# x's first four tiles updated ahead of the last output half's copy, and the norm sums ahead of the spectrum products

## What is computed

```python
for l in range(DEPTH):                                   # DEPTH = 2
    h = rms_norm(x, norm1) * (1 + sc1) + sh1
    ... = split(h @ w_in)                                # attention, Hyena and retention branches
    # Hyena: long convolution with a filter that depends on weights alone
    filt = hyena_filter(...); y = irfft(rfft(u) * rfft(filt))
    x = x + g1 * (merged @ w_out)
    h2 = rms_norm(x, norm2) * (1 + sc2) + sh2
    x = x + g2 * moe(h2, ...)                            # top-1 group, top-2 of its 4 experts
y = rms_norm(x, final_g)
```

## Time and profile before

| | us |
|---|---|
| median of 3 runs | 1156.74 (1155.05 to 1159.61) |
| profiled execution, first to last instruction (span) | 1155.5 |
| TensorE busy in it | 1100.4 (95%) |
| VectorE busy | 542.0 (47%) |
| ScalarE busy | 209.8 (18%) |

### The profile page before, as it was taken

One profiled execution on the slowest core, in us unless ns is written; L12 is line 12 of the kernel. 1 busy time (PEld: TensorE's weight loads), 2 busy tenths in 40 slices (PEclk: granted clock), 3 DMA queues, 4 the chain that ended last, 5 costly groups with the idle time before them and its releaser, 6 DMA issues.

```text
span 1155.5 us, 15668 instructions
## 1 busy us (share of the span) xinstructions
PE 1100.4 (95%) x6026; PEld 783.7 (68%) x6026; DVE 542.0 (47%) x1202; ACT 209.8 (18%) x440; POOL 41.0 (4%) x83
## 2 busy tenths in 40 slices
PE   6999999999999999999889999999999999999965
PEld 4688888878887445454358888888888844545422
DVE  2469887677846311121244886646543551111003
ACT  3251022232021101111025111323201210000001
POOL 1001110000000000000000111000000000000000
PEclk9999999999998999999999999999999899999999
DMA  9657865467587999999955677437347979999993
GB/s 382 284 204 279 326 221 227 168 270 272 219 350 318 419 420 422 420 421 421 421 219 201 215 276 285 174 133 283 139 145 306 375 305 421 421 420 421 421 420 121
DMA packets 56943, 351.38 MB, mean 304 GB/s; under 512 B 7088, under 2 KB 7264, under 8 KB 20512
## 3 DMA queue, kind: packets, MB, share of 16 engines
q1 hardware_dynamic: 52704, 337.75, 73.5%
q0 software_dynamic: 4160, 12.58, 3.0%
HBM read 346.08 MB, written 2.65 MB: 302 GB/s over the span
## 4 chain that ended last, share of the span: by engine, by line
PE 84%; DMA 8%; DVE 3%; SPq 3%; ACT 1%; issue 1%; DVEq 0%; ACTq 0%
PE bank L836 26%; PE bank L1127 15%; PE bank L1016 7%; PE bank L1148 6%; DMA ring<-in_experts 5%; PE bank L1037 5%; PE bank L831 5%; PE bank L1112 5%; PE bank L1169 3%; PE bank L847 3%; DMA ring<-in_weights 3%; SPq L615 2%; PE bank L760 1%; PE bank L820 1%; PE bank L961 1%
## 5 line engine op out<-in xcount | busy, mean ns | idle before, releaser
L836 PE MATMUL bank<-h,ring 128*128 128x256 f32 x1472 | 324.8, 380 | 0.0
L836 PEld LDWEIGHTS bank<-h,ring 128*128 128x128 f32 x1472 | 277.4, 190 | 40.1 <-issue 3.2
L1750 DVE SCALAR_TENSOR_TENSOR ring<-ring 128x1024 f32<-128x1024 f32 x160 | 189.5, 1222 | 18.7 <-DMA ring<-in_mod_weights 9.1
L1127 PE MATMUL bank<-ring,gates 128*32 128x512 f32 (+2 forms) x616 | 137.7, 614 | 8.8 <-DMA h<-in_experts 5.0
L1127 PEld LDWEIGHTS bank<-ring,gates 128*32 128x32 f32 (+2 forms) x616 | 41.2, 126 | 69.5 <-issue 69.1
L1127 PE MATMUL bank<-lent,gates 128*32 128x512 f32 (+2 forms) x408 | 81.4, 593 | 2.0 <-ACTq L1618 2.0
L2238 DVE COPY uc_zt_dsum<-bank 128x512 f32<-128x512 f32 x14 | 9.7, 692 | 122.8 <-PE bank L1148 122.8
L1148 PE MATMUL bank<-ring,gates 128*32 128x512 f32 (+1 forms) x240 | 64.4, 595 | 2.0 <-issue 1.2
L1148 PE MATMUL bank<-lent,gates 128*32 128x512 f32 (+2 forms) x304 | 60.5, 594 | 1.3 <-DMA ring<-in_experts 1.0
L1112 PE MATMUL bank<-uc_zt_dsum,gates 128*128 128x128 f32 x448 | 55.5, 285 | 1.0 <-DVEq L2246 1.0
L1127 PEld LDWEIGHTS bank<-lent,gates 128*32 128x32 f32 (+2 forms) x408 | 25.2, 123 | 46.2 <-issue 43.7
(11 more groups left out here) (271 smaller groups left out, 1203.7 us busy)
## 6 DMA issues: line engine op xcount, KB each, us to landing
ring<-in_experts SPq DMA_DIRECT2D x93, 1024.0 KB, 19.8
ring<-in_weights SPq DMA_DIRECT2D x85, 1024.0 KB, 7.7
lent<-in_experts SPq DMA_DIRECT2D x72, 1024.0 KB, 17.8
ring<-in_mod_weights SPq DMA_DIRECT2D x80, 512.0 KB, 5.1
h<-in_experts SPq DMA_DIRECT2D x10, 1024.0 KB, 19.4
uc_zt_dsum<-in_experts SPq DMA_DIRECT2D x10, 1024.0 KB, 19.5
va_vr<-in_experts SPq DMA_DIRECT2D x7, 1024.0 KB, 12.2
lent<-in_weights SPq DMA_DIRECT2D x3, 1024.0 KB, 23.5
```

What stands on the lines that cost most here:

```text
L836: last = pe.matmul(bank[b][:, c * TOK:(c + 1) * TOK], w[:, k, c * P:(c + 1) * P], h[:, k, :], start=(k == 0), stop=(k == KT - 1))
L1127: last = pe.matmul(bank[b][rows, :], hgat[:, 4 * half + f, rows], w[j][:, f, :], start=(half == 1 and f == 0), stop=(half == 0 and f == 3) ...
L1750: last = dve.scalar_tensor_tensor(out, w, 0.5, cond_wide[:, c, :], ALU.mult, ALU.mult, accum_out=mod_all[:, of, row, c:c + 1])
```

## The change

There are three edits. On TensorE, `norm_sum(1)` directly follows the last combine of layer 0; the first two pairs of spectrum products stand behind it, and the third behind `first_units`. On VectorE, x's updates move ahead of the jump, and those of banks 0 and 1 ahead of the copy of the last output half. For this the blocks of further experts, which add to banks 0 to 3 later, start their sums afresh (`True` in place of `False`) and update x once more each; their semaphore counts six events in place of five. The counts of `s_bank_free` for banks 0 to 3 now come ahead of the jump, too.

```diff
+            def spectrum_sum(layer, b, taps_cos, taps_back):
+
+                pe.wait_ge(s_taps, 2 * layer + 2)
+                take(b)
+                pe.matmul(bank[b][:, :], C(taps_cos), hs[:, 0, :], start=True, stop=False)
+                pe.matmul(bank[b][:, :], C(taps_back), hs[:, 1, :], start=False,
+                          stop=True).then_inc(s_spectrum_sum, 1)
...
                 else:
+                    spectrum_sum(layer, 5, "cf", "cf1")
+                    spectrum_sum(layer, 6, "s0", "s1")
                     first_units(layer)
+                    spectrum_sum(layer, 7, "nq", "nq1")
...
                 on = nc.switch_bb(f"pe_on{layer}")
-                if layer + 1 < DEPTH:
-                    filter_step(layer + 1, 4)
             norm_sum(DEPTH)
...
-                        for b in range(4, 8):
+                        for b in range(8):
                             pe.wait_ge(s_bank_free[b], taken[b])
...
-                out_high(PAIRS)
+
+                def moved(b):
+
+                    src = tiles(b)
+                    for c in range(2):
+                        t = 2 * b + c
+                        for g in range(GROUPS):
+                            last = stt(x[:, t, g_cols(g)], src[:, c, g_cols(g)],
+                                       mod_all[:, layer, 40 + t, g:g + 1], x[:, t, g_cols(g)], ALU.mult,
+                                       ALU.add)
+                    return last
+
+                for b in range(4):
+                    if b == 2:
+                        out_high(PAIRS)
+                    dve.wait_ge(s_combined, combined(layer, PAIRS + b + 1))
+                    moved(b).then_inc(s_x_moe, 1)
+                for b in range(4):
+                    dve.wait_ge(s_x_moe, 4 * layer + b + 1)
+                    dve.sem_inc(s_bank_free[b], 1)
...
                     dve.wait_ge(s_more_combined[layer], n + 1)
+                    for b in range(4):
+                        link(moved(b))
+                    dve.sem_inc(s_more_by_vector[layer], 1)
...
                 on = nc.switch_bb(f"dve_on{layer}")
-                for b in range(4):
-                    dve.wait_ge(s_combined, combined(layer, PAIRS + b + 1))
-                    src = tiles(b)
-                    for c in range(2):
-                        t = 2 * b + c
-                        for g in range(GROUPS):
-                            last = stt(x[:, t, g_cols(g)], src[:, c, g_cols(g)],
-                                       modT[:, 40 + t, g:g + 1], x[:, t, g_cols(g)], ALU.mult,
-                                       ALU.add)
-                    last.then_inc(s_x_moe, 1)
-                for b in range(4):
-                    dve.wait_ge(s_x_moe, 4 * layer + b + 1)
-                    dve.sem_inc(s_bank_free[b], 1)
```

More of the change, by code:

```diff
@@ L333, in trunk_program @@
         s_more_known = sem("more_known")
-        s_more_by_vector = [sem(f"more_picked_hgat_act_actT_y{n}") for n in range(DEPTH)]
+        s_more_by_vector = [sem(f"more_picked_hgat_act_actT_y_moved{n}") for n in range(DEPTH)]
         s_more_used = [sem(f"more_used{n}") for n in range(DEPTH)]
@@ L1183, in loaded @@
                     return more[part % 2]
-                pe.wait_ge(s_more_by_vector[layer], 5 * n + 1)
+                pe.wait_ge(s_more_by_vector[layer], 6 * n + 1)
                 for g in range(GROUPS):
@@ L1193, in more_block @@
                 last.then_inc(s_more_gathered[layer], 1)
-                pe.wait_ge(s_more_by_vector[layer], 5 * n + 2)
+                pe.wait_ge(s_more_by_vector[layer], 6 * n + 2)
                 for part in range(4):
@@ L1200, in more_block @@
                     last.then_inc(s_more_used[layer], 1)
-                pe.wait_ge(s_more_by_vector[layer], 5 * n + 3)
+                pe.wait_ge(s_more_by_vector[layer], 6 * n + 3)
                 for f in range(4):
@@ L1204, in more_block @@
                 last.then_inc(s_more_turned[layer], 1)
-                pe.wait_ge(s_more_by_vector[layer], 5 * n + 4)
+                pe.wait_ge(s_more_by_vector[layer], 6 * n + 4)
                 for part in range(4, 6):
@@ L1211, in more_block @@
                     last.then_inc(s_more_used[layer], 1)
-                last = combine(s_more_by_vector[layer], 5 * n + 5, s_more_by_vector[layer],
-                               5 * n + 5, s_more_by_vector[layer], scat[0], False)
+                last = combine(s_more_by_vector[layer], 6 * n + 5, s_more_by_vector[layer],
+                               6 * n + 5, s_more_by_vector[layer], scat[0], True)
                 last.then_inc(s_more_combined[layer], 1)
+                pe.wait_ge(s_more_by_vector[layer], 6 * n + 6)
             pe.wait_ge(s_ones_set, 2)
@@ L1368, in more_block @@
             def more_block(layer, i):
-                sc_e.wait_ge(s_more_by_vector[layer], 5 * i + 1)
+                sc_e.wait_ge(s_more_by_vector[layer], 6 * i + 1)
                 e = sc_e.value_load(ints[0:1, 1:2], min_val=0, max_val=N_EXPERTS - 1)
@@ L1382, in more_block @@
                     s_more_tanh[layer], 1)
+                sc_e.wait_ge(s_more_by_vector[layer], 6 * i + 6)
             sc_e.wait_ge(s_shared_in, 16)
```

## The result

| | before | changed |
|---|---|---|
| median of 6 runs, us | 1155.19 (1154.36 to 1159.61) | 1149.45 (1148.37 to 1152.93) |
| ratio, 95% interval | | 0.9944, 0.9927 to 0.9961 |
| profiled execution, span | 1155.5 | 1148.3 |

The medians differ by 5.7 us; the forecast was 5.9. The time forecast was 1150.9 us and 1149.45 was measured: the gain fits, and the 1.45 us between the two come from the starting point, since the median before is 1.55 us lower over these six runs (1155.19) than over the three that the forecast started from (1156.74). The ratio stands for 6.5 us with an interval of 4.5 to 8.4, and two later groups of runs of the same kernel gave 0.9938 (0.9922 to 0.9953) and 0.9942 (0.9930 to 0.9954). The two profiled executions differ by 7.2 us, which is more than the sum, so the profile has to say where.

What follows compares the result with a forecast made beforehand. Bound: the chain through the seam between layers, where TensorE idles 4.05 us and its clock then falls. 3.43 + 1.69 + 0.74 = 5.86 us off the 1155.5 span, plus 1.2 around it: 1150.9 us, range 1147.9 to 1154.2.

Steps and rivals of the forecast that it cites:

- the sum: Whole kernel: the gains of order, clock and early updates together, 5.86 us.
- The seam: Between the layers, last combine of layer 0 to layer 1's third unit: 25.0 us instead of 30.1.
- C: Rival at the seam: the idle stretch costs more than in this profile, so more is gained; 1149.6 us, chance 0.12.
- B: Rival at the seam: the clock falls anyway; gain 4.2 us, time 1152.6, chance 0.13.
- the clock: Layer 1's first projections: full clock, because TensorE idles about 0.8 us instead of 4.05; gain 1.69 us.
- the order: Seam: norm sums follow the combine, two product pairs fill the norm's stretch, the third costs 1.72; gain 3.43 us.
- The early updates: End of layer 1: x's first updates ahead of the copy bring the norm's mean earlier; gain 0.74 us.
- Edit 3: VectorE's jump and bank waits between the updates' end and the mean; hidden today, no gain or loss in the total.
- E: Rival at the seam: the compiled order puts a wait before the norm sums; gain 1 to 3, 1154.7 us, chance 0.04.
- F: Rival, slower: the early updates hold up the last half's copy in each layer; chance 0.04.
- D: Rival in layer 1's experts: the DMA stream takes back the seam's gain, only 0.74 left; 1156.0 us, chance 0.09.
- the line of 0.5%: Whole kernel: 5.8 us, about what a measurement can tell from no change; the forecast gain sits on it.

Runs made afterwards that it cites:

- experiment 4: Kernel before plus 16 matmuls with unread results between the norm sums and layer 1's first two units; 1153.78 us against 1156.56, ratio 0.9983.
- Experiment 3: Changed kernel with all three pairs of spectrum products behind the first two units; 1156.69 us against 1156.56 for the kernel before, ratio 1.0002.
- experiments 1: Kernel before with only TensorE's new order, x's updates left behind the copy and the jump; 1151.64 us against 1156.56, ratio 0.9964.
- experiments 2: Changed kernel with the spectrum products back in front of the norm sums; 1155.81 us against 1156.56 for the kernel before, ratio 0.9993.
- experiment 5: Changed kernel with ten unread VectorE operations ahead of the last half's copy in both layers; 1152.08 us against the changed kernel's 1149.59.
- experiment 7: Changed kernel with the third pair's products, one each, in TensorE's waits for the last weights and the copy; 1149.85 us, run again 1147.25.
- its variant: Changed kernel with both products of the third pair in TensorE's wait for VectorE's copy; 1147.01 us, ratio to the kernel before 0.9924.

## Why the prediction was right

**The seam.** Forecast 25.0 us from the combine to the third unit, measured 25.08, 25.07 and 25.07. The bounds of the range follow from their sums only to 0.2 us (C's 1149.6 less 1.5 is 1148.1, not 1147.9; B's 1152.6 and 1.5 are 1154.1), which changes nothing. The seam's two terms stand apart in the experiments: the clock 1.69 forecast, 1.62 measured (experiment 4); the order 3.43, which is left of 5.05 when the clock's 1.62 is taken off. That the two fit to 0.01 is partly chance, since the clock's part was 1.4 to 1.7 us in the profiles with the idle stretch. Experiment 3 shows the reason that was given for the order's part, the two pairs in the stretch of the norm.

**The clock.** The granted clock is 1.00 in the first units wherever TensorE's idle time ahead of them is 0.5 to 0.6 us (changed kernel, experiments 1 and 4) and lower wherever it is 4.05 (before, experiments 2 and 3). The Trainium skill in "TensorE: Matmul & The Clock Gate", section "A second HAM failure mode: psum-queue depth-cycling", tells of a bf16 kernel in which frequent brief idle times make the clock swing between its two levels. That is not borne out at this seam, whose matmuls are fp32: the changed kernel has three of 0.7 to 0.9 us and one of 0.6 within 18 us and the clock is 1.00. But the prediction's reading that stretches of this length leave the clock alone holds for the seam only. In the routing stage the clock falls where TensorE was idle for just 0.21 us in the 22 us ahead (last section), so the length of an idle stretch does not decide alone.

**The early updates.** 0.74 forecast at the end of layer 1, 0.74 or 0.75 in every profile that has the edit. One number was off: I let the early updates start at 577.6, at the end of the whole combine, where bank 0 is closed halfway through it. They start 1.14 us behind its start, so their cover was 3.05 us and not 2.4. The miss was to the safe side and no term hung on it. Edit 3, the branch behind the updates, was not run by itself. It costs nothing that shows: at both places the norm sums start 1.80 or 1.81 us behind the combine, and the mean comes 5.46 us behind it, as without hindrance.

**The rivals.** B, the clock falling anyway: refuted by the 1.00 in every profile of the changed kernel. C, an idle stretch that costs more than in the first profile: not seen, the two other profiles that have it (experiments 2 and 3) lose 1.4 and 1.7 us by it. E, a wait ahead of the norm sums: they start 1.80 us behind the combine, so there is none. F, the copy held up: its wait is 0.90 us as before. D, the DMA stream taking it back: refuted. TensorE still sets when the stream of the experts' weights restarts in layer 1: its first issue comes 3.70 us behind the first expert matmul before (930.92 and 927.22) and 3.69 with the change (924.23 and 920.54). The waits of SyncE in the changed kernel, 890 to 1000 us, answer to the earlier trace rows:

```profile
SPq L615 <- PE bank L1132: 40.9, 12, 11.8
...
SPq L613 <- PE bank L1093: 10.9, 1, 10.9
```

The longest wait is 11.8 us in place of 16.1, because the last pieces ahead of it are issued later in the stage; they wait for the turning of the tokens (L1088 before, L1093 changed), whose 32 records took 3.82 us before and 6.43 in this execution, where the clock was lower. And in the twelve profiles the time from the third unit of layer 1 to its last combine, less the stage of the routing, lies between 505.0 and 505.4 us (experiment 5 without its 1.14), whatever the seam took: 505.24 before, 505.22 changed.

**What is above the sum.** The ratios stand for 6.5, 7.2 and 6.7 us, the sum for 5.9 (a ratio of 0.9949), which lies inside all three intervals, each time in their upper part. The stage of the routing is where executions differ. From the router's first matmul to the first expert matmul of layer 1 the twelve profiles have 19.6 to 22.2 us for the same work. The timeline of PE in the two extremes, first the kernel of experiment 7, then its variant:

```profile
898.34 1.85 PE L1069 MATMUL bank<-shd,h 128*128 128x16 f32 x16
...
914.00 4.05 PE L1124 MATMUL bank<-uc_zt_dsum,gates 128*128 128x128 f32 x32 [1.03 <-DVEq L2268]
917.98 6.23 PE L1139 MATMUL bank<-ring,gates 128*64 128x512 f32 x28
```

```profile
898.17 1.85 PE L1069 MATMUL bank<-shd,h 128*128 128x16 f32 x16
...
913.73 6.72 PE L1124 MATMUL bank<-uc_zt_dsum,gates 128*128 128x128 f32 x32 [1.03 <-DVEq L2267]
920.38 4.08 PE L1139 MATMUL bank<-ring,gates 128*64 128x512 f32 x18
```

The windows at the end of that stage, the kernel of experiment 7 and then its variant, have the granted clock at 1.00 and at 0.72:

```profile
908.00:918.00 10.00, 8.39 (x71) 7.76 (x70) 7.77 (x26) 0.00 (x0) 0.00 (x0) 1.00 0.62 236
```

```profile
908.00:920.40 12.40, 10.88 (x70) 10.41 (x68) 8.37 (x29) 0.00 (x0) 0.00 (x0) 0.72 0.47 188
```

The 32 records of L1124 take 4.05 us at clock 1.00 and 6.72 where it is lower. In windows of half a microsecond all twelve profiles show the clock at 0.50 somewhere in this stage. Four have it early alone, within 11 us of the router's first matmul, and they take 19.6 to 20.5 us. The other eight have it (alone or once more) behind 12 us, where these 32 records stand, and take 20.8 to 22.2. The changed kernel's three profiles have 20.4, 20.5 and 20.8 us there, the three with a seam of 30 us 21.4, 20.9 and 20.8. Experiment 5, which has the changed kernel's seam, has 21.4. Whether the shift of the work makes the fall cheaper on the average, by half a microsecond, or whether this is chance, stays open: so few profiles do not tell. The difference between the sum's 5.9 and the ratios' 6.5 to 7.2 us is thus not explained, only not distinguished from scatter. The prediction had put the change on the line of 0.5% (0.48 for faster to 0.47 for the same); the interval, 0.39 to 0.73%, contains that line, and the runs do not decide it either. Of the 7.2 us between the two first profiles, 1.0 is this stage and 0.6 lies ahead of the seam, where the two programs do the same; there the profiles scatter by more than that (the router of layer 0 starts at 347.7 to 350.8).

## What to carry to other kernels

When a chain of small steps on other engines stands ahead of the next big matmuls, look what independent work stands in TensorE's stream before that chain's start, and put as much of it as fits behind it: each microsecond of it in the gap was gained here (3.43 us), and where the empty gap of 4 us had lowered the clock, 1.6 more. Merely moving the chain forward gave nothing in a kernel whose TensorE is busy for 95% of the time (experiment 3). Work that does not fit in one wait can be cut to the size of others. A wait for another engine's copy, which was 0.89 to 0.91 us at the seam in every profile that had nothing put in front of it, is a safer place than a wait for a DMA, which was anything from 0 to 0.87.

## What the runs showed of the hardware

Sixteen useless matmuls made the kernel 2.0 us faster (0.6 to 3.4, experiment 4), by keeping the clock up: 13.89 us for 64 records in place of 15.51. And the clock falls not only behind idle stretches: in layer 1's routing the window of 898 to 908 has TensorE busy for 9.62 of 9.83 us in the variant's profile, at a mean granted clock of 0.83:

```profile
898.17:908.00 9.83, 9.62 (x72) 9.52 (x71) 5.85 (x29) 2.92 (x7) 0.00 (x0) 0.83 1.01 419
```

What TensorE does there are the router's matmuls (128x16) and the turning of the tokens (128x128). In finer windows of the same profile the clock is 1.00 up to 902, 0.50 from 903 to 906 and 1.00 again from 907. In the 22 us ahead of the fall TensorE was idle for 0.21 us in all, between the two groups of the router's small matmuls. What brings the fall there is not shown. Every profile has such falls in this stage, at different places, so that a stage of 20 us differs by up to 2.6 us between executions of kernels that do the same in it.
